# A two-layer hybrid decoder step: first expert round as straight code, another buffer order for the expert weights, and a rearranged outset

## The reference

```python
proj = x @ w_in[l]                      # 1024 -> 5632 columns
# (A) pooling mixer, (B) gated conv of width 31, (C) conv of width 4 and RG-LRU times GeLU
merged = sum(sigmoid(gate_b + b_gate) * (branch_b @ w_br_b) for b in 3 branches)
x = layer_norm(ALPHA * x + merged @ w_out[l])
# layer 0: dense SwiGLU, d_ff 2816;  layer 1: top-2 of 8 experts, SwiGLU, d_expert 3584
x = layer_norm(ALPHA * x + ffn(x))
```

## Time and profile before

| | |
|---|---|
| median of 3 runs | 1525.67 us (1519.15 to 1527.46) |
| the profiled execution | 1522.57 us |
| its span, first to last instruction | 1520.4 us |
| PE busy | 1415.5 us, 93% |
| PE weight loads busy | 1157.1 us, 76% |
| DVE busy | 1344.1 us, 88% |
| ACT busy | 1109.9 us, 73% |
| POOL busy | 106.5 us, 7% |
| moved by transfers | 464.91 MB, mean 306 GB/s |

### The profile page before, as it was taken

One profiled execution on the slowest core, in us unless ns is written; L12 is line 12 of the kernel. 1 busy time (PEld: TensorE's weight loads), 2 busy tenths in 40 slices (PEclk: granted clock), 3 DMA queues, 4 the chain that ended last, 5 costly groups with the idle time before them and its releaser, 6 DMA issues.

```text
span 1520.4 us, 40894 instructions
## 1 busy us (share of the span) xinstructions
PE 1415.5 (93%) x17642; PEld 1157.1 (76%) x17642; DVE 1344.1 (88%) x1433; ACT 1109.9 (73%) x1069; POOL 106.5 (7%) x155
## 2 busy tenths in 40 slices
PE   6999999999999999899989999999899889798786
PEld 4788887888887888598687797788787775766672
DVE  3898998546569899899999999999999999999995
ACT  3796765434448776588797878889888887978883
POOL 3031013000043001200000000000000000000001
PEclk9999999999999999999999999999999999999997
DMA  9744375456544437699999999999999999999992
GB/s 297 271 142 151 139 254 194 153 167 236 194 178 139 167 111 270 231 413 348 407 413 387 412 411 381 412 407 382 412 406 411 411 406 411 411 402 410 411 395 78
DMA packets 141204, 464.91 MB, mean 306 GB/s; under 512 B 8086, under 2 KB 10262, under 8 KB 126652
## 3 DMA queue, kind: packets, MB, share of 16 engines
q1 hardware_dynamic: 139100, 457.47, 78.7%
q0 software_dynamic: 1760, 4.50, 1.0%
q10 hardware_dynamic: 160, 0.27, 0.1%
HBM read 460.79 MB, written 2.89 MB: 305 GB/s over the span
## 4 chain that ended last, share of the span: by engine, by line
PE 52%; DVE 24%; issue 15%; ACT 4%; DMA 2%; POOL 1%; SPq 1%; DVEq 0%; ACTq 0%
PE ps L825 16%; PE ps L826 16%; PE ps L827 16%; DVE w_lo L2188 10%; DVE w_lo L2191 6%; PE ps L930 2%; DMA stage<-in_w_in 2%; ACT w_hi L1294 1%; ACT w_hi L1590 1%; DVE arena L2204 1%; DVE arena L2223 1%; DVE z L2178 1%; POOL x L755 1%; DMA out_lconv_s<-in_state_lru_conv 1%; DVE z L1679 1%
## 5 line engine op out<-in xcount | busy, mean ns | idle before, releaser
L825 PE MATMUL ps<-arena,w_hi 128*128 128x128 f16 (+7 forms) x3952 | 566.4, 214 | 28.4 <-issue 11.3
L826 PE MATMUL ps<-arena,w_hi 128*128 128x128 f16 (+7 forms) x3952 | 566.5, 214 | 15.8 <-issue 15.7
L827 PE MATMUL ps<-arena,w_lo 128*128 128x128 f16 (+7 forms) x3952 | 566.5, 214 | 11.7 <-issue 11.7
L825 PEld LDWEIGHTS ps<-arena,w_hi 128*128 128x128 f16 x3952 | 386.3, 99 | 40.4 <-issue 16.9
L827 PEld LDWEIGHTS ps<-arena,w_lo 128*128 128x128 f16 x3952 | 386.4, 99 | 23.5 <-issue 17.8
L826 PEld LDWEIGHTS ps<-arena,w_hi 128*128 128x128 f16 x3952 | 386.4, 99 | 21.8 <-issue 14.0
L825 PE MATMUL ps<-xhl,w_hi 128*128 128x264 f16 x1120 | 312.6, 279 | 8.8 <-ACT arena L1428 3.6
L826 PE MATMUL ps<-xhl,w_hi 128*128 128x264 f16 x1120 | 312.5, 279 | 0.0
L827 PE MATMUL ps<-xhl,w_lo 128*128 128x264 f16 x1120 | 312.3, 279 | 0.0
L1662 DVE SCALAR_TENSOR_TENSOR w_lo<-stage,w_hi 128x2048 f16<-128x2048 f32 (+1 forms) x96 | 213.0, 2239 | 89.9 <-ACT w_hi L1294 89.6
L1294 ACT ACTIVATE w_hi<-stage 128x2048 f16<-128x2048 f32 (+1 forms) x96 | 176.5, 1852 | 99.4 <-PE ps L827 76.1
(11 more groups left out here) (335 smaller groups left out, 1957.9 us busy)
## 6 DMA issues: line engine op xcount, KB each, us to landing
stage<-in_moe_w_down SPq DMA_DIRECT2D x64, 1024.0 KB, 14.2
stage<-in_moe_w_gate SPq DMA_DIRECT2D x48, 1024.0 KB, 9.1
mixer_only<-in_moe_w_up SPq DMA_DIRECT2D x48, 1024.0 KB, 13.3
stage<-in_w_in SPq DMA_DIRECT2D x44, 1024.0 KB, 5.7
stage<-in_moe_w_up SPq DMA_DIRECT2D x32, 1024.0 KB, 13.2
arena<-in_moe_w_gate SPq DMA_DIRECT2D x32, 1024.0 KB, 13.4
x<-in_moe_w_up SPq DMA_DIRECT2D x16, 1024.0 KB, 13.6
mixer_only<-in_moe_w_gate SPq DMA_DIRECT2D x16, 1024.0 KB, 13.0
```

Source lines behind the costliest of these rows:

```text
L825: mm(out, ah, bh, start=start, stop=False, skip_group_check=True)
L826: mm(out, ah, bl, start=False, stop=False, skip_group_check=True)
L827: return mm(out, al, bh, start=False, stop=stop, skip_group_check=True)
```

## The change

**Straight code.** The first round's eight visits stand one after the other, without a loop. Then each of PE, ACT and DVE compares `nr` with 2. If it is less, the end of the kernel follows at once; the further rounds are a loop in the `Else` branch, with a copy of the end behind it. The small `If` blocks of visit 7 are gone. The engine waits of the first round compare with constants.

**The ring's order.** Places 0 to 11 are followed by places 0 to 4 once more (`TWICE`), and only then by 12 and 13. So pieces 12 to 16 go to the stage slots as soon as pieces 0 to 4 are split, and pieces 17 and 18 wait for x and the logits. Any place still comes round every 14 pieces.

**The outset.** The sample rows and ten parameter transfers are issued by ACT, the other five by POOL, all at the start. Piece 0 is loaded and split in two halves. PE runs 22 matmuls on constants before x is there, transposes four blocks of x, uses piece 0, and transposes the other four blocks before piece 1. POOL waits for piece 1 instead of x's second half, and loads only layer 0's states; those of layer 1 and the router follow after the first layer norm, and PE transposes them between the up and the down projection of the dense feed-forward.

The core of the diff (DVE's end is moved into `token_norms` in the same way as ACT's; `hi_v`, `lo_v` and the gathers are only taken out of `visit`):

```diff
+TWICE = 5
+RING_ORDER = list(range(TWICE, 12)) + list(range(TWICE)) + [12, 13]
...
-                for l_ in range(L):
-                    for h in range(2):
-                        put(("st_conv", l_, h))
-                    put(("st_pool", l_))
-                    put(("st_lru", l_))
+                for h in range(2):
+                    put(("st_conv", 0, h))
+                put(("st_pool", 0))
+                put(("st_lru", 0))
...
+            for h in range(2):
+                put(("st_conv", 1, h))
+            put(("st_pool", 1))
+            put(("st_lru", 1))
...
+        def home_of(n):
+
+            p = n - PRE
+            if p < TWICE:
+                return p, 0
+            h = RING_ORDER[(p - TWICE) % RING]
+            return h, (p - TWICE) // RING + (h < TWICE)
+
         def home(n):
 
-            return stage[:, n % SLOTS, :] if n < PRE else HOMES[(n - PRE) % RING]
+            return stage[:, n % SLOTS, :] if n < PRE else HOMES[home_of(n)[0]]
 
         def landed(n, r=0):
 
-            i, turn = (n - PRE) % RING, (n - PRE) // RING
-            if n < PRE or i < SLOTS:
-                first = n // SLOTS if n < PRE else (PRE + i) // SLOTS + turn
-                return stage_full[(n if n < PRE else PRE + i) % SLOTS], r * (16 * ROUND // RING) + 16 * (first + 1)
-            return stage_full[i], r * (16 * ROUND // RING) + 16 * (turn + 1)
+            if n < PRE:
+                return stage_full[n % SLOTS], 16 * (n // SLOTS + 1)
+            h, turn = home_of(n)
+            if h < SLOTS:
+                slot = (PRE + h) % SLOTS
+                return stage_full[slot], r * (16 * ROUND // RING) + 16 * ((PRE + h) // SLOTS + turn + 1)
+            return stage_full[h], r * (16 * ROUND // RING) + 16 * (turn + 1)
 
...
-            sp.dma_start(xs_rows[0:NS_, :], A["x_sample"].rearrange("b s n -> (b s) n")).then_inc(S["ld_x"], 16)
...
-            def small_vectors():
-                for i, name in enumerate(VEC_B):
...
-                    sp.dma_start(pard_rows[(3 + i) * L:(4 + i) * L, :], A[name]).then_inc(S["ld_par"], 16)
-
-            for n in range(PRE):
-                if n == 3:
...
+            src = pre_piece(0)[0]
+            dst = home(0).rearrange("p (k n) -> p k n", k=4)
+            sp.dma_start(dst[:, 0:2], src[:, 0:2]).then_inc(S["ld_first"], 16)
+            sp.dma_start(dst[:, 2:4], src[:, 2:4]).then_inc(stage_full[0], 16)
+            sp.dma_start(x_rows[:, :, 512:D], rows[:, :, 512:D]).then_inc(S["ld_x2"], 16)
+            for n in range(1, PRE):
...
-                        if first and v == 0 and m < RING:
+                        if first and v == 0 and m < RING + TWICE:
...
-                elif m == 12:
+                elif 12 <= m < 12 + TWICE:
+                    sp.wait_ge(S["lo_done"], split(PRE + m - 12 + 1))
+                elif m == 12 + TWICE:
                     filled(sp, ("xtok", 2, 1))
                     sp.wait_ge(S["z_start"], KT)
-                elif m == 13:
+                elif m == 13 + TWICE:
...
-            pool.wait_ge(S["ld_x2"], 16)
...
+            pool.dma_start(pard_rows[0:3 * L, :], A["b_gate"].rearrange("l (b n) -> (l b) n", b=3)).then_inc(S["ld_pard"], 16)
+            for i, name in enumerate(VEC_D):
+                pool.dma_start(pard_rows[(3 + i) * L:(4 + i) * L, :], A[name]).then_inc(S["ld_pard"], 16)
+
+            def states(l):
...
+            pool.wait_ge(stage_full[1], 16)
+            states(0)
...
                 if l == 0:
+                    states(1)
+                    pool.dma_start(w_rt[:, :, :], A["moe_router"][0].rearrange("(k p) n -> p k n", p=P)
+                                   ).then_inc(S["ld_small"], 16)
...
+            pe.wait_ge(S["dve"], 1)
+            for _ in range(22):
+                mm(bank(("xT", 7))[:, 0:2 * P], ones_d[:, :].bitcast(F16)[:, 0:P], ones_b[:, :].bitcast(F16),
+                   start=True, stop=True, skip_group_check=True)
+
+            def turned(ks):
+                for k in ks:
+                    o = bank(("xT", k))
+                    for a in range(2):
+                        nc.tensor.transpose(o[:, a * P:(a + 1) * P], x_rows[:, a, k * P:(k + 1) * P], ident)
+                    nc.tensor.transpose(o[:, TP:T], xs_rows[0:NS_, k * P:(k + 1) * P],
+                                        ident[0:NS_, 0:NS_]).then_inc(full_of(("xT", k)), 1)
+
             pe.wait_ge(S["ld_const"], 16)
             pe.wait_ge(S["ld_x"], 32)
-            for k in range(KT):
-                if k == 4:
-                    pe.wait_ge(S["ld_x2"], 16)
...
-                        if as_landed(n):
+                        if n == 0:
+                            pe.wait_ge(S["first_lo"], 1)
+                        elif as_landed(n):
                             pe.wait_ge(*landed(n))
                         else:
+                            if n == 1:
+                                pe.wait_ge(S["ld_x2"], 16)
+                                turned(range(4, KT))
                             pe.wait_ge(S["lo_done"], split(n + 1))
...
-                                rows_half(slot, names_, half, 512, lambda kk: read_out(pe, ("xT", kk)))
+                                def first(kk):
+                                    if kk == 2:
+                                        pe.wait_ge(S["lo_done"], 1)
+                                    read_out(pe, ("xT", kk))
+
+                                rows_half(slot, names_, half, 512, first)
                             else:
...
+                    states(1)
...
+            def last_visit(at):
+
                 up_to_gather(at)
                 down(at, NB - 1)
                 residual_rows(2, [in_visit(bank_free, b, at, PER_VISIT[b] - 1) for b in (0, 2)])
...
+            def token_rows_out(nv):
+
+                cap = CAPS[NE - 1]
+                for h in range(2):
+                    pe.wait_ge(*in_visit(bank_free, 4 + h, nv, -1))
+                    for i in (0, 2, 1):
+                        n = P if i < 2 else NS_
+                        b = TOKEN_BANK[i, h]
+                        mm(ps[0:n, b, :], onehot_t[0:cap, i * P:i * P + n], yh[0:cap, h * 512:(h + 1) * 512],
+                           start=False, stop=False, skip_group_check=True)
+                        mm(ps[0:n, b, :], onehot_t[0:cap, i * P:i * P + n], yl[0:cap, h * 512:(h + 1) * 512],
+                           start=False, stop=True, skip_group_check=True).then_inc(bank_full[b], 1)
+
+            visit((0, 0), True)
+            for v in range(1, NE - 1):
+                visit((0, v))
+            pe.wait_ge(S["visits_ready"], 1)
+            nr = pe.value_load(visits_i[0:1, 0:1], min_val=1, max_val=ROUNDS)
+            last_visit((0, NE - 1))
+
+            with pe.If(nr < 2):
+                token_rows_out((1, 0))
+            with pe.Else():
+                with pe.Fori(1, nr) as r:
+                    gather((r, 0), (r - 1, NE - 1))
+                    for v in range(NE - 1):
+                        visit((r, v))
+                    last_visit((r, NE - 1))
+                token_rows_out((nr, 0))
...
+            act.dma_start(xs_rows[0:NS_, :], A["x_sample"].rearrange("b s n -> (b s) n")).then_inc(S["ld_x"], 16)
+            for i, name in enumerate(VEC_B):
+                act.dma_start(par_rows[i * L:(i + 1) * L, :], A[name]).then_inc(S["ld_par"], 16)
+            r = len(VEC_B) * L
+            act.dma_start(par_rows[r:r + L * CW, :], A["conv_w"].rearrange("l k n -> (l k) n")).then_inc(S["ld_par"], 16)
+            r += L * CW
+            act.dma_start(par_rows[r:r + L * LW, :], A["lru_conv_w"].rearrange("l k n -> (l k) n")).then_inc(S["ld_par"], 16)
 
             for k in range(KT):
                 filled(act, ("xT", k))
                 fn(xh[:, k, :], bank(("xT", k))[:, 0:T], ACT.Copy).then_inc(S["x_hi"], 1)
+                if k == 1:
+                    act.wait_ge(S["ld_first"], 16)
+                    fn(w_hi[:, 0, 0:PIECE // 2], home(0)[:, 0:PIECE // 2], ACT.Copy, scale=WS).then_inc(S["first_hi"], 1)
                 if k == 3:
-                    hi(0)
+                    act.wait_ge(*landed(0))
+                    fn(w_hi[:, 0, PIECE // 2:], home(0)[:, PIECE // 2:], ACT.Copy, scale=WS).then_inc(S["hi_done"], 1)
             for n in range(1, AHEAD):
                 hi(n)
...
+            def next_round(at):
+                next_tokens(at)
+                for m in range(VISIT, VISIT + SLOTS):
+                    hi_v(at, m)
+
...
+            for v in range(NE - 1):
+                visit((0, v))
             act.wait_ge(S["visits_ready"], 1)
             nr = act.value_load(visits_i[0:1, 0:1], min_val=1, max_val=ROUNDS)
-            with act.Fori(0, nr) as r:
...
+            visit((0, NE - 1))
+
+            with act.If(nr < 2):
+                token_norms((1, 0))
+            with act.Else():
+                with act.Fori(1, nr) as r:
+                    next_round((r - 1, NE - 1))
```

(11 more changed lines are left out.)

365 lines of the change are left out of this document (162 added, 203 removed).

## The result

The changed kernel takes 1514.22 us (median of 8 runs, 1512.26 to 1514.95) against 1522.84 for the kernel before (8 runs, 1519.15 to 1528.56). The ratio is 0.9938 with a 95% interval of 0.9924 to 0.9952: by the ratio 9.4 us less (by the medians 8.6), where 9.2 was forecast, with 6.2 to 11.7 as the range. (The forecast of 1516.5 is on the scale of the earlier three executions with their median of 1525.67; only differences compare.) In a second group, on another occasion, the same pair gave 0.9947 (0.9930 to 0.9964). The profiled execution took 1512.99 us (before: 1522.57), with a span of 1511.0 (before: 1520.4).

What follows compares the result with a forecast made beforehand. Engines were taken to bound the expert part to about 1340, transfers after. Outset 5.5 + states 0 + ring 0 + end 3.7 = 9.2 us: 1513.4 against the profiled execution, 1516.5 on the median's scale; range 1509 to 1523.

Steps and rivals of the forecast that it cites:

- The bound of each stage: Engines hold the expert part to about 1340, transfers after; gains before 640 reach the end, transfer-only gains 620 to 1045 do not.
- Piece 5: Outset: less load on POOL's queue lands this weight piece 4.0 us earlier, so PE resumes at 39.0, not 43.0.
- The two terms of the estimate: For piece 5's landing: 1.9 us less slowdown from POOL's queue plus 2.1 us of plain transfer for 0.8 MB.
- The clock: Outset, behind the sigmoid's wait: PE arrives without a long rest, so 14 matmuls avoid half pace; 1.5 us won.
- The states: Layer 1's transposes moved from about 54 to about 380: 1.8 us won, 1.8 lost, nothing; bounds -1.8 and 0.
- The ring: Before the first expert visit, 620 to 630: five pieces land up to 20 us sooner, worth 0; bounds -1 and +1.5.
- The end: PE's last matmuls: the 2.03 us rest goes and twelve matmuls keep the faster pace; 3.7 us won, bounds 0 and 4.
- The sum: Whole kernel: 5.5 + 0 + 0 + 3.7 = 9.2 us won.
- (b): Rival, outset: small rows issued at once delay x and piece 0 by 3 us; sum 4.7, 1521.0; chance 0.20.
- (c): Rival, end: PE's jump costs the same whichever side is taken, no gain there, 1520.2; chance 0.08.
- (d): Rival, outset without rest: 22 matmuls bring full pace, piece 5 lands at 33; sum 13.7, 1512.0; chance 0.14.
- (e): Rival, slower: PE rests before piece 1, half pace throughout pieces 0 to 2; 1531.5, if piece 1 starts after 29; chance 0.06.

Runs made afterwards that it cites:

- run 2: The changed kernel with the ring's old order (TWICE = 0, places 0 to 13 in sequence); 0.9952 of the kernel before.
- run 3: The changed kernel with layer 1's states and the router issued in the outset again, and those states' transposes early again; 0.9976 of the kernel before.
- run 6: The changed kernel with the small parameter rows issued by SP again, behind piece 2; 0.9944 of the kernel before.
- run 11: The changed kernel with five transfers of small pooling and gate matrices held on POOL's queue until piece 8 has landed; 0.9919 of the kernel before, 1512.86 us.
- run 5: The kernel before with only PE's program in the new straight form, the rows' matmuls right behind the comparison; 0.9966 of the kernel before.
- run 1: The changed kernel measured again without any edit, in a second group; 0.9947 of the kernel before.
- run 4: The changed kernel with only PE's end in the old form, loop over rounds and untaken block back; 0.9966 of the kernel before.
- run 7: The changed kernel without the 22 matmuls on constants ahead of x; 0.9938 of the kernel before.
- run 8: The changed kernel with ACT's table load and first four sigmoids ahead of its copies of pieces 4, 5 and 6; 0.9952 of the kernel before.
- run 9: As run 8, with PE also turning x's second half inside piece 0, ahead of its last quarter of inputs; 0.9948 of the kernel before.

## Why the prediction was right, and where only by luck

**The bound of each stage** was read rightly. What was won ahead of 640 reached the end (the lead is 4.2 at 645 and 5.4 at yl), what the ring won on the transfers between 615 and 640 did not, the hole at 1045 stayed, and ACT's waits did not change (run 2). One number in the prediction is misnamed: its "8.3 us of waiting and slow stretches" is the sum of the two waits alone (4.7 and 3.6). It enters no sum.

**Piece 5** was forecast 4.0 us earlier and came 4.8 earlier; the sigmoid 3.6 forecast (39.0), 4.7 measured. Run 3 shows that the load of POOL's queue is the cause, run 6 that the small rows have no part in it, and run 11 continues it by 2.3 us for 0.5 MB. The 0.8 us between forecast and result say nothing: the old outset landed the piece at 40.1 in one profile and at 38.8 in another (run 5), the changed one between 35.0 and 36.2 in six. The two terms of the estimate, the slowdown and the plain transfer, were not told apart.

**The clock** is the step that the runs leave to chance: "PE arrives at the sigmoid's wait with no long rest before it, so I count the 1.5 us as won". In the profiled pair it failed. PE had the first half of piece 2 done at 34.4, where 37 to 39 was forecast, and so stood for 3.9 us as before; behind that, 25 matmuls ran at half pace where 14 had, and in place of 1.5 won, 1.2 were lost. But in six profiles piece 5 lands and ACT's order is as in the changed kernel, and they fall into two kinds (us; a slow stretch is one with a granted clock of 0.50):

| profile | piece 5 lands | slow stretch from 22 to 24 on | PE at the sigmoid's wait | its wait | slow stretch behind it | lead at 111 |
|---|---|---|---|---|---|---|
| the result's | 35.3 | 3.4 | 34.4 | 3.9 | 6.8 | 5.2 |
| run 1 | 35.6 | 3.4 | 35.0 | 3.5 | 6.8 | 4.9 |
| run 6 | 35.4 | 3.4 | 34.5 | 3.8 | 6.8 | 5.2 |
| run 2 | 35.7 | 6.8 | 36.7 | 1.9 | none | 7.4 |
| run 4 | 36.2 | 6.8 | 37.3 | 1.9 | none | 6.9 |
| run 7 | 35.0 | 6.8 | 36.2 | 1.7 | none | 8.0 |

PE's wait for the sigmoid in run 2, to be held against the 3.9 of the result:

```profile
PE ps L841 <- ACT arena L1483: 1.9, 1, 1.9
```

Where the slow stretch at piece 1 is the longer one, PE comes later to a wait that ends by ACT all the same, so it loses nothing there, rests less, and keeps the full pace behind. In these three the 1.5 us were won, and PE was there near the 37 that was forecast. Run 1, without an edit, is of the first kind, and runs 2 and 4, whose edits lie near 620 and at the end, are of the second. So it is no edit that decides between them; what does stays open. The parts of the outset without the states' move come to 3.1 to 3.4 us in three profiles and to 5.1 to 6.2 in the other three, where 5.5 was forecast, all against one profile of the old outset, which itself can be 1.3 better (run 5). So the earlier landing was forecast rightly, and the 1.5 us for the clock come or not by chance.

**The states** were costed at -1.8 and +1.8. They measured +1.8 in the outset and -1.7 in the feed-forward. Both ends are full stretches of PE, so nothing is left.

**The ring** at nothing: right (run 2), by the mechanism given.

**The end**: 3.7 forecast, 4.1 measured, 3.97 with PE's code alone (run 5). The place, PE's rest with the branch in it, and the next bound, DVE's sums, were right. Whether the rest is the jump over the untaken block or the loop's end beside it was not told apart; both went together. The twelve matmuls kept a pace of 0.22, but with 3.2 us from first start to last end and not 2.6, since at four places between them the next starts 0.3 behind and not 0.2; DVE covered it. The Trainium skill's rule on taken branches ("Runtime: NRT & Kernel Launch", section "Instruction fetch mechanics") would have put a new jump at the end of every engine; the span ends 9.4 us earlier, as DVE's last result does (9.5), so if there is such a jump, it is covered by the last store, and the trace agrees with the sum, not with a loss. No run shows the jump by itself.

**The sum** of 9.2 met 9.4, and part of that is luck. In the profiled pair the terms of the forecast come to 3.5 + 0 + 0 + 4.1 = 7.6 us. The further 1.9 us are differences in later places which no step had named: the clock at 117 and at 632 (+1.7, -1.0), a shorter wait at 478 (+0.7), the transfer-bound end (+1.2) and what was not traced (-0.6). With the other kind of outset the same terms would come to 9.2 to 10.3. The two groups' ratios, 9.4 and 8.1 us, lie between 7.6 and 10.3.

**The rivals.** (b), the small rows spoil the outset: half right. Issued at the start they do hold up what lands beside them: x's second half came at 14.0 and piece 1 at 18.2, where run 6 has 10.3 and 13.0. But nothing hung on it: in both the result's profile and run 6 PE began piece 1 at 23.7 after 4.6 us of rest, which the chain over the late transposes, ACT's copies and DVE's remainder sets. (c), the jump costs the same: refuted by the trace. (d), the outset without rest, came in no run: run 8 took away the wait for the sigmoid and run 9 also shortened the rest before piece 1 to 3.15, and neither shows a gain, since DVE and ACT are late next, up to 46 and 83. Nor did the 22 matmuls bring piece 0 to full pace in the result's profile: PE rested 2.0 us behind x's first half and ran the first 12 matmuls at 0.22. (e), slow throughout: the rest before piece 1 was 4.6 us, in the span named, but piece 1 started between 23.7 and 26.1 in the six profiles, well ahead of the point 29, and the slow level there ended within 6.8 us.

## What to carry to other kernels

A wait at the head of the list may be worth nothing or little: before removing it, follow the chain to the next thing that is late, here a landing, and ask what shares the way with it. Small transfers that nobody needs yet cost the large ones ahead of which they stand; moving 0.8 MB of them behind the last urgent piece brought it 4.4 to 4.8 us forward (run 3), moving another 0.5 MB 2.3 more (run 11). A lead read from one pair of profiles can be 2 us of chance: in this outset the same edits gave 4.9 to 8.0 us at one and the same place. And an untaken block with a loop's end, placed between the last matmuls, gives PE a rest at the one place where nothing covers it (with the slower pace behind it 4.0 us, run 5).

## What the runs showed of the hardware

The granted clock falls after the same rest in one execution and not in the next; what decides it stays open. After PE's rest of 2.0 us at about 110 it was at 0.50 in 7 of the 14 profiles and untouched in 7; after the one at about 475 (1.9 to 3.2 us) in 8 of 14; after the one of 2.0 us at about 503 in none; after the one of 3.3 to 3.5 us at 632 in 13, all but the one where it was filled. A fall lasted 3.4 or 6.8 us and cost half of that where PE was full: the lead rises by 1.67 behind 117.7, where only the kernel before was slow for 3.4 us. Two windows over the same work, the kernel before and then the changed one:

```profile
110.00:150.00 40.00, 38.01 (x323) 32.22 (x322) 32.38 (x52) 27.54 (x40) 6.63 (x7) 0.96 0.53 172
...
110.00:150.00 40.00, 37.99 (x339) 32.82 (x337) 34.89 (x58) 27.50 (x42) 6.61 (x7) 1.00 0.50 159
```

So two profiles of the changed kernel have spans of 1511.0 and 1513.1 with nothing changed, and a step of the lead must be checked against the clock of its window before it is put down to an edit.

With the untaken block and the loop's end in between, PE stood for 1.98 to 2.03 us (run 4); the form with the rows right behind the comparison left no such rest in any of its twelve profiles.

Transfers of one and the same outset land over 1 us apart from one execution to the next (piece 5 at 40.1 and 38.8 in the old one, at 35.0 to 36.2 in the changed one). While POOL's queue carried 1.83 MB of the 3.52 MB between 16 and 30, the core moved 251 GB/s; between 34 and 50, with that queue idle, 385.
